# Modulation sums by transposes and folds, an earlier first modulation, and head sums in two quarters of the array

## The reference

```python
# first block
mod = silu(c) @ w_ada + b_ada;  shift, scale, gate = split(mod, 3)      # w_ada 1024 x 3072
h = rms_norm(x, norm_gain) * (1 + scale) + shift
q_a, k_a, v_a, z_a, q_b, kc, vc, ks, vs, kw, vw, z_b, g_b = split(h @ w_in)
# heads of 64 channels; every q and k head is normed: t * rsqrt(mean(t*t over 64) + eps) * gain
# o_a: 8 heads, window of 128 keys, distance bias, sinks
# o_b: 8 heads, compressed + selected + window branches, mixed by sigmoid gates
x = x + gate * (concat(o_a * silu(z_a), o_b * silu(z_b)) @ w_out)
# second block, two layers
mod = silu(c_2) @ ada_w[i] + ada_b[i]                                   # 1024 x 6144 per layer
# layer 0: differential attention over x and 256 context rows (modulated by silu(c_ctx) @ ada_w[0])
# layer 1: short convolution; each layer ends with a SwiGLU of width 2816
```

## Time and profile before

| | |
|---|---|
| median of 3 runs (lowest, highest) | 1791.21 us (1784.34, 1792.2) |
| the profiled execution's own time | 1788.7 us |
| its span, mean granted TensorE clock | 1786.9 us, 0.972 |
| TensorE matmul busy | 1720.8 us (96%) |
| VectorE (DVE) busy | 976.8 us (55%) |
| ScalarE (ACT) busy | 679.1 us (38%) |

### The profile page before, as it was taken

The page is one execution under the profiler, slowest core; times in us unless marked ns, Lnnn a source line. Parts: engine busy times, 40 slices in busy tenths (PEclk is TensorE's granted clock), DMA queues, the critical chain, the costliest instruction groups (busy, mean ns, idle before and its releaser), DMA issues.

```text
span 1786.9 us, 23061 instructions
## 1 busy us (share of the span) xinstructions
PE 1720.8 (96%) x8968; PEld 1411.6 (79%) x8968; DVE 976.8 (55%) x1803; ACT 679.1 (38%) x1417; POOL 61.2 (3%) x119
## 2 busy tenths in 40 slices
PE   4899999999999999899999999999999899999999
PEld 2777777777999999777788887887888788888887
DVE  4666466666866776666555554346555533333232
ACT  3434555554545555554222222223222422222221
POOL 0000000000000000000000000000000000000000
PEclk8899997899999999998999999998999999999999
DMA  8886332212223131221666555432443233333332
GB/s 302 218 244 162 97 92 86 71 37 72 65 60 99 45 99 44 83 61 38 188 187 184 174 175 156 121 109 84 120 125 97 71 95 94 95 94 95 97 110 77
DMA packets 290215, 202.02 MB, mean 113 GB/s; under 512 B 76247, under 2 KB 272072, under 8 KB 289082
## 3 DMA queue, kind: packets, MB, share of 16 engines
q1 hardware_dynamic: 266942, 133.21, 26.5%
q0 software_dynamic: 15536, 56.37, 10.5%
q10 hardware_dynamic: 7628, 10.97, 1.8%
HBM read 197.33 MB, written 5.28 MB: 113 GB/s over the span
## 4 chain that ended last, share of the span: by engine, by line
PE 88%; DVE 6%; ACT 2%; issue 2%; DMA 2%; ACTq 1%; SPq 0%; DVEq 0%
PE PS L858 13%; PE PS L859 13%; PE PS L860 13%; PE PS L841 5%; PE PS L842 4%; PE PS L840 4%; PE PS L1283 3%; PE PS L1285 3%; PE PS L1284 3%; PE PS L1088 3%; PE PS L1333 2%; PE PS L1357 2%; PE PS L1062 2%; PE PS L1070 1%; PE PS L1345 1%
## 5 line engine op out<-in xcount | busy, mean ns | idle before, releaser
L2014 DVE TENSOR_TENSOR WL<-WS,WH 128x512 fp32r<-128x512 f32 x416 | 268.3, 687 | 269.7 <-ACT WH L1506 269.2
L1506 ACT ACTIVATE WH<-WS 128x512 fp32r<-128x512 f32 x416 | 237.7, 621 | 182.5 <-PE PS L842 140.4
L858 PE MATMUL PS<-A3H,WL 128*128 128x512 f32 x672 | 267.3, 398 | 0.0
L859 PE MATMUL PS<-A3L,WH 128*128 128x512 f32 x672 | 266.5, 397 | 0.0
L860 PE MATMUL PS<-A3H,WH 128*128 128x512 f32 x672 | 264.2, 393 | 0.0
L858 PEld LDWEIGHTS PS<-A3H,WL 128*128 128x128 f32 x672 | 126.2, 188 | 33.5 <-issue 2.8
L860 PEld LDWEIGHTS PS<-A3H,WH 128*128 128x128 f32 x672 | 126.2, 188 | 31.0
L859 PEld LDWEIGHTS PS<-A3L,WH 128*128 128x128 f32 x672 | 126.2, 188 | 28.9
L841 PE MATMUL PS<-GL,WH 128*128 128x512 f32 x352 | 139.7, 397 | 0.0
L840 PE MATMUL PS<-GH,WL 128*128 128x512 f32 x352 | 139.0, 395 | 0.4 <-DVE WL L2014 0.4
L842 PE MATMUL PS<-GH,WH 128*128 128x512 f32 x352 | 139.3, 396 | 0.0
(11 more groups left out here) (362 smaller groups left out, 3506.8 us busy)
## 6 DMA issues: line engine op xcount, KB each, us to landing
AW<-in_ada_w POOLq DMA_DIRECT2D x96, 512.0 KB, 4.2
WS<-in_ffn_w_gate_up SPq DMA_DIRECT2D x88, 512.0 KB, 4.2
WS<-in_ffn_w_down SPq DMA_DIRECT2D x32, 512.0 KB, 4.1
WS<-in_sc_w_in SPq DMA_DIRECT2D x24, 512.0 KB, 3.9
AB<-in_w_ada SPq DMA_DIRECT2D x8, 1024.0 KB, 16.0
WS<-in_w_in SPq DMA_DIRECT2D x32, 256.0 KB, 4.3
WS<-in_diff_w_qkv SPq DMA_DIRECT2D x64, 128.0 KB, 2.6
WS<-in_ffn_w_down SPq DMA_DIRECT2D x16, 384.0 KB, 3.4
```

Source lines behind the costliest of these rows:

```text
L858: mm(PS[:, b, :], wl[:, k, :], hi[:, k, 0:S], start=(k == 0), stop=False)
L859: mm(PS[:, b, :], wh[:, k, :], lo[:, k, 0:S], start=False, stop=False)
L1506: f(weights(p)[0][:, k, :], WS[:, p % 2, k, :], ACT.Copy).then_inc(w_hi, 1)
L2014: tt(lo[:, k, :], WS[:, p % 2, k, :], hi[:, k, :].bitcast(F32), ALU.subtract).then_inc(w_lo, 1)
```

## The change

The first w_ada columns are loaded by GpSimd in two blocks of 2 x 512 columns, sixteen loads of 512 KB, once all small rows are in. DVE sums block 0, then block 1, splits the kcvc panels, and takes M1 and the norm's scale in halves, with four tiles of the norm after each. TensorE sums each block over partitions by itself (banks 6 and 5). ACT copies US and splits the kcvc panels ahead of the norm. The two `distance_table` copies move from ACT's DMA queue to SP's, between the loads of z0 and z1.

In attention, e, g and h sums are made by 8 transposes in two small jobs of 4 (128 columns each), and DVE folds each group of 512 columns with one reduction and adds the bias (`fold_sums`); five more small jobs come in, and e0 and its kind start one step earlier. In up0 the four sums are made by 8 transposes into banks 5 and 6 and one reduction of 1024 columns. `head_sum` is two matmuls, each of 64 rows and 64 columns.

```diff
 def head_sum(a, u, n, cols=S, of=None):
     pe.wait_ge(sq_ready, a.norm(n) + 1)
     bank = take_small(a, u)
-    mm(bank[:, 0:cols], BLK if of is None else of, SQ[:, (a.n0 + n) % 2, 0:cols],
-       start=True, stop=True).then_inc(small_done, 1)
+    for g in range(2):
+        r = slice(g * HD, (g + 1) * HD)
+        m = mm(bank[r, 0:cols], BLK[r, r], SQ[r, (a.n0 + n) % 2, 0:cols], start=True, stop=True)
+    m.then_inc(small_done, 1)
...
+def turn_sums(name, n, sums, half):                      # attention: e, g, h
+    pe.wait_ge(part_sum, sums_before(n + 1))
+    bank = take_small(att, att_small(name))
+    for f in range(4):
+        c = (4 * half + f) * P
+        m = tp(bank[:, f * P:(f + 1) * P], sums[:, c:c + P], IDENT)
+    m.then_inc(small_done, 1)
+def fold_sums(u, v, dst, read, c):                       # DVE
+    dve.wait_ge(small_done, att.small(u) + 1)
+    dve.tensor_reduce(FOLD[:, c:c + 4], PS[:, SIDE, :].rearrange("p (f k) -> p f k", k=P), AX.X, ALU.add)\
+        .then_inc(small_free, 1)
+    dve.wait_ge(small_free, att.small(u) + 1)
+    m = tt(dst[:, c:c + 4], FOLD[:, c:c + 4], VT[:, V_ADAB + v + c:V_ADAB + v + c + 4], ALU.add)
+    m.then_inc(read if c else part_fold, 1)
+def turn_layer_part(a, u, n):                            # up0, passes 5, 9, 13, 17
+    pe.wait_ge(part_sum, sums_before(n + 1))
+    take_small(a, u)
+    for f in range(KT):
+        m = tp(FLAT[:, FOLD_BANK * S + f * P:...], AA[:, n % 2, f * P:(f + 1) * P], IDENT)
+    m.then_inc(small_done, 1)
...
 # SP
-for k in range(KT):
-    sp.dma_start(AB[:, k, :], w_ada[k, :, 0:2 * D]).then_inc(ada_loaded[k], 16)
...
     head_pair(a, j, (ZB if j >= 4 else ZA) * P + j % 4 * HD)
+    if j == 0:
+        sp.wait_ge(rows_out, 16)
+        for head, at, n in ((0, 3 * P - 1, 2 * P), (8, P - 1, S)):
+            sp.dma_start(dist_table[head:head + 8, :, 0:n], ...).then_inc(dist_out, 16)
 # GpSimd
+pool.wait_ge(vec_in, 16 * len(small_rows()))
+for b in range(2):
+    for k in range(KT):
+        pool.dma_start(block_of_ada(AB[:, k, :], b), block_of_ada(w_ada[k, :, 0:2 * D], b))\
+            .then_inc(ada_loaded[4 * b + k // 2], 16)
 # TensorE, stage ada_a
+for b in range(2):
+    pe.wait_ge(ada_used, KT * (b + 1))
+    for half in range(2):
+        for f in range(4 * b, 4 * b + 4):
+            m = mm(PS[:, 6 - b, KT * half + f:...], AA[:, half, f * P:(f + 1) * P], ONES[:, 0:1], ...)
+    m.then_inc(ada_summed, 1)
 # ACT: ahead of the x tiles
+for k in range(2):
+    act.wait_ge(small_done, a.small(2 + k) + 1)
+    f(US[:, k * 320:(k + 1) * 320], PS[0:16, SMALL, 0:320], ACT.Copy).then_inc(small_free, 1)
 # ACT: after the write of distance_rows
-act.wait_ge(rows_out, 16)
-for head, at, n in ((0, 3 * P - 1, 2 * P), (8, P - 1, S)):
-    act.dma_start(dist_table[head:head + 8, :, 0:n], ...).then_inc(dist_out, 16)
+for j in range(2):
+    split(At("kcvc"), j)
 load_set(LN_AND_EXP)
-layer_norm("norm_a", 0, A1H, slice(0, S), M1, first_panels=At("kcvc"))
+layer_norm("norm_a", 0, A1H, slice(0, S), M1)
 # DVE
+dve.wait_ge(cs_ready, 1)
+add_ada(0)
+add_ada(1)
+split(At("kcvc"), 0)
+split(At("kcvc"), 1)
+dve.wait_ge(ln_rs, 1)
+for b in range(2):
+    take_ada(b)                     # M1 and NS of four tiles each, from bank 6 - b
+    layer_norm(0, None, H, A1H, A1L, ..., tiles=range(4 * b, 4 * b + 4))
```

More of the change, by code:

```diff
@@ L348, in hybrid_then_diff_conv @@
         EPSC = sb("EPSC", [P, 1])
+        FOLD = sb("FOLD", [P, 8])
         SM = sb("SM", [P, 64])
@@ L784, in _ @@
             pool.memset(EPSC[:, :], EPS).then_inc(eps_set, 1)
+            w_ada = ins["w_ada"][0].rearrange("(k p) n -> k p n", p=P)
+            pool.wait_ge(vec_in, 16 * len(small_rows()))
[3 more added lines that the diff above has]
+                        .then_inc(ada_loaded[4 * b + k // 2], 16)
             pool.wait_ge(cs_ready, 1)
[L787 removed]
+            pool.wait_ge(ada_added, 2)
             pool.wait_ge(rows_out, 16)
@@ L946, in _ @@
             add_square(KT - 1)
[L947 to L954, removed]
+            for b in range(2):
+                pe.wait_ge(ada_used, KT * (b + 1))
+                for half in range(2):
+                    for f in range(4 * b, 4 * b + 4):
+                        m = mm(PS[:, 6 - b, KT * half + f:KT * half + f + 1], AA[:, half, f * P:(f + 1) * P], ONES[:, 0:1],
+                               start=True, stop=True)
+                m.then_inc(ada_summed, 1)
             a = At("kcvc")
@@ L1133, in att_small_work @@
                 kind, j = name[0], name[1:]
[L1134 to L1143, removed]
+                if name[0] in "egh":
+                    n, sums = {"e0": (1, AA[:, 1, :]), "e1": (1, AC), "g0": (2, AA[:, 0, :]), "g1": (2, AC), "h0": (3, AA[:, 1, :])}[name[0:2]]
+                    turn_sums(name, n, sums, 1 if name[2:] else 0)
                 elif name == "lam":
@@ L2115, in _ @@
                 copy(VT[:, k * P:(k + 1) * P], PS[:, SMALL, 0:P]).then_inc(small_free, 1)
-            for k in range(2):
-                dve.wait_ge(small_done, a.small(2 + k) + 1)
-                copy(US[:, k * 320:(k + 1) * 320], PS[0:16, SMALL, 0:320]).then_inc(small_free, 1)
+            dve.wait_ge(cs_ready, 1)
[6 more added lines that the diff above has]
+                take_ada(b)
+                layer_norm(0, None, H, A1H, A1L, slice(0, S), M1[:, 8:16], M1[:, 0:8], V_NG, 0, tiles=range(4 * b, 4 * b + 4))
+            a = At("mods1")
             dve.wait_ge(small_free, a.small(0) + 1)
@@ L2484, in take_layer_part @@
             def take_layer_part(stage, u, n, bank=None):
+                dve.wait_ge(small_done, At(stage).small(u) + 1)
+                c, src = 8 * (n - 1), FOLD[:, :]
                 if bank is None:
[L2487 to L2491, removed]
+                    dve.tensor_reduce(src, FLAT[:, FOLD_BANK * S:(FOLD_BANK + 2) * S].rearrange("p (f k) -> p f k", k=P), AX.X,
+                                      ALU.add).then_inc(part_fold, 1)
+                    dve.wait_ge(part_fold, 5 + u + 1)
+                else:
+                    src = PS[:, bank, 0:8]
+                tt(M2[:, c:c + 8], src, VT[:, V_ADAB + c:V_ADAB + c + 8], ALU.add).then_inc(part_read, 1)
                 dve.wait_ge(part_read, n + 1)
```

83 lines of the change are left out of this document (40 added, 43 removed).

## The result

The changed kernel takes 1793.45 us (median of 16 runs, 1785.91 to 1798.72), the kernel before beside it 1785.82 us (16 runs, 1777.51 to 1793.86). The ratio is 1.0031, with a 95% interval of 1.0019 to 1.0044: some 5.5 us slower. That is less than the 0.5% that the prediction took as the least difference to tell from none, but the interval lies above 1, and the forecast (1779 us) was the other way. The profiled execution took 1796.1 us at the same mean clock, 0.972.

A forecast was written before the change was run, and what follows sets the result against it. TensorE, its matmuls busy for 96% of the span, was taken as the bound; -2 - 4.4 - 3.5 + 1 + 2 - 4.6 = -11.5 us took 1788.7 to 1777.2, and 2.5 for the median gave 1779 us, range 1771 to 1787.

The forecast's parts named there:

- The start: AB's loads by GpSimd, last pair in at 35.5 to 36 us, gain mostly given back as z1 waits: -2 us.
- Sums: Eight transposes replace sixteen one-column products, 0.88 us saved per sum on TensorE: -4.4 us in attention, -3.5 in up0.
- DVE's fold: Longer reductions on DVE for attention's sums, nearly all hidden since TensorE looks ahead two steps: +1 us.
- The bound of +6.5: Upper bound for the cost of DVE's longer reductions in attention, +1.3 us per sum: +6.5 us; lower bound 0.
- rival 4: DVE or ACT sets attention's pace and TensorE's time saved there turns idle: 1788 us, chance 0.08.
- Head sums: In attention, two half-array products run side by side, with two mode changes of 0.1 us per head sum: +2 us.
- rival 2: The two head products run one after the other, as both write one PSUM bank: +9.5 us, 1789 us, chance 0.13.
- The clock: In attention, transposes instead of one-column products give back part of the low-clock time behind e1, g0 and g1: -4.6 us.
- The prediction's mark for failing: The prediction as a whole fails if attention, 173 to 420 us before, is not at least 4 us shorter.
- Rival 3: At the start, GpSimd's software queue is slow, AB's sixteen loads taking 3 us each: 1805 us, chance 0.07.
- rival 1: At the start, the table copies don't hold up z1, so the start gives -7.7 us: 1773 us, chance 0.10.

The follow-up runs named there:

- the unused tile: The kernel before with FOLD, 32 bytes per partition, declared in its place in memory and used by nothing: 1783.61 us, ratio 0.9975.
- the combination: The kernel before with e and g by folds, h0 old, up0's four sums by folds with DVE's reduction behind the next two splits: 1770.78 us, 0.9897.
- start alone: The kernel before with only the start's edits (AB by GpSimd, kcvc split early, table copies in SP's queue): 1800.87 us, ratio 1.0059.
- weights held: The kernel before with the start's edits, but SP issues kcvc and W2 only when AB's first block has landed: 1793.86 us, ratio 1.0037.

## Why the prediction was wrong, by its steps

**The start (-2; measured +10 to +11): the step that failed.** "AB's loads ... begin at 14.5 us, the last pair is in at 35.5 to 36": it was in at 45.8 us. The rate was right: the eight pairs of 1 MB landed from 27.6 to 45.8 us, one every 2.6 us, 400 KB per us. But a pair is in only with the slowest of the DMA engines. The fastest had their last pieces by 38 us, 2 over the forecast, AB's packets having begun at 16.1 us; the slowest had its last at 45.8. What I left out is what now stands ahead of AB: the panels of kcvc and W2, which I counted as a gain ("both kcvc panels now land early") and not as packets on the engines that AB needs. The pieces of the first pair landed from 18.3 to 27.6 us, and DVE, which needs 2.6 us for a pair as well, could not catch up. DVE ended at 51.2 instead of 41.0. The second half was right: from z0's issue to z1's split I had 23 us (40 to 63), and it took 22.8 (50.0 to 72.8), with z1 right behind the copies. But I gave the hold-up against a gain that did not come; the two together are the loss, 8.2 to 8.3 us at full clock. z3 then needed 11.32 us, as before.

**Sums (-4.4 and -3.5): right in TensorE's time, wrong in the net.** A sum takes 0.9 us less. DVE's fold I had at +1 for "TensorE looks ahead two steps"; but all small jobs share bank 1, and a job takes it only when the one before has been read out. DVE comes late to the fold, behind its other work, and the next job now stands close behind. 6.0 us of waits in attention eat the 4.4, and in up0 four times 0.7 eat most of the 3.5, since the next panel's split stood behind the reduction on DVE. At full clock, against the unused tile, attention's folds cost 2.2 us and up0's gain 0.3. The bound of +6.5 was DVE's added busy time, and that the waits come near it is chance. The mechanism is rival 4's, by a thing that I did not name, the single bank.

**Head sums (+2): right, though the timed runs hide it.** The records run two by two and take 1.00 us instead of 0.86: 11 x 0.14 = 1.5 us; rival 2 is out. The timed pairs say -2 us (0.9989, alone), +4 (in the changed kernel) and +7 (0.9938 against 0.9897, in the combination), and no constant cost fits all three. At full clock it is +3.1, +2.4 and +0.6 us, each within 1.3; the rest is the clock. Whether the head sums move the clock is not shown. The Trainium skill ("TensorEngine Tiling (Array Packing)", Restrictions and Gotchas) says that different row tiles can't access one PSUM bank simultaneously; four records of two row halves into one bank, pairwise at one time, in 1.00 us where one after the other is 1.7, don't agree with it, and the measurement decides here.

**The clock (-4.6): not shown.** Behind e1 the low stretch is gone, and around g0 and g1 (274 to 301 us) three of 3.4 us stand for one of 13.7 and two of 3.4. But the unused tile, without any fold, has as little low time from 173 to 355 us, so the sums need not be the cause. At h0 13.7 us at 1.2 GHz stand behind 2.5 us of new idle time, where the unused tile has 10.2. Over all its runs the clock took 2.0 us less from the changed kernel, within 2.5. It took 4 to 11 us less from the five kernels that are the kernel before with e and g by folds and h0 not crowded, but also 4.3 less from the head sums alone, so the cause stays open.

**What I did not have at all** is the 32 bytes, 5 us faster. Without them the changed kernel would be some 10 us slower than before. At full clock the parts alone add up to 9.2 us (start 8.3, tile -4.1, attention 2.2, up0 -0.3, head sums 3.1), and 6.5 were measured: they add up only roughly. The prediction's mark for failing, attention not 4 us shorter, is met: from 173 to 420 us it is 1.5 us longer. Rival 3 had the point of turning right (block 1 in at 45 us, measured 45.8) by luck and with the wrong reason: the software queue was not slow, it was late and shared. Its sum and rival 1's add 1.8 us to 1788.7, which already holds them; nothing hangs on that.

## What to carry to other kernels

When a load moves to another queue, write down what stood behind it and now runs ahead of it or beside it; small packets on shared DMA engines delay it on the slowest engine, and it is that one that counts. When a short operation becomes a longer one on an engine with much idle time, look at the resource that it holds meanwhile and at the next item behind it: placing the reduction behind the splits brought 3 us that its price alone hid. Before a gain is put down to an edit, look at stages that the edit doesn't touch, and take span x clock of all timed runs beside their times: here it told differences of 1 to 2 us where the times, moved by the clock, could not.

## What the runs showed of the hardware

A shift of later tiles in memory by 32 bytes changes the distance of matmul groups in dense stages from 0.7000 to 0.6971 us, in all twelve kernels here that have it and in none of the five that haven't. The first and the last piece of AB's first pair landed 8.8 us apart beside small packets (start alone, 19.1 and 27.9 us), and 2.6 us apart without them (weights held, 18.9 and 21.5). Two 64 x 64 products at the diagonal of the array, into one bank, ran at one time: four records in 1.00 us. Runs of one kernel differed by 1.5 to 5.6 us (standard deviation) in what the clock took, and by 0.8 to 2.5 in span x clock.
